# One stage of a two-block transformer kernel: running sums as rows by transfer instead of by matrix products, and another order of the work around them

## What is computed

```python
z, xbc, dt_raw, q, k, v, f_raw, g_ssd, g_att = split(h @ w_in)
# branch 1: chunked state-space product, 16 heads, 4 groups, chunk L = 128, two chunks
xbc = silu(conv(xbc)); xs, bm, cm = split(xbc); dt = softplus(dt_raw + dt_bias)
a_cs = cumsum(dt * A)                                  # within a chunk, per head
decay = exp(where(causal, a_cs[l] - a_cs[s], -inf))    # 128 x 128 per head and chunk
y_diag = ((cm . bm) * decay) @ (x * dt)
states = bm' @ (x * dt * exp(a_cs[-1] - a_cs));  y_off = (cm @ prev) * exp(a_cs)
y = y_diag + y_off + d_skip * x
y_ssd = (rms(y * silu(z)) * ssd_norm_w) @ w_ssd_o
# branch 2: forgetting attention, 8 heads of 64, query blocks of 128
F = cumsum(log_sigmoid(f_raw + forget_b))
o = softmax(q.k / 8 + F[t] - F[s], s <= t) @ v;  y_att = o @ w_att_o
out = (sigmoid(g_ssd) * y_ssd + sigmoid(g_att) * y_att) @ w_o
```

## Time and profile before

| | |
|---|---|
| median of 3 runs (lowest, highest) | 2125.88 us (2124.75, 2131.48) |
| the profiled execution, its time | 2127.87 us |
| its span, first to last instruction | 2126.1 us |
| TensorE busy | 1608.8 us, 76% of the span |
| VectorE, ScalarE, POOL busy | 419.5, 284.0, 60.2 us |
| bytes moved | 670.53 MB, mean 315 GB/s |
| mean granted TensorE clock | 0.875 of full speed |

### The profile page before, as it was taken

The page is one execution under the profiler, slowest core; times in us unless marked ns, Lnnn a source line. Parts: engine busy times, 40 slices in busy tenths (PEclk is TensorE's granted clock), DMA queues, the critical chain, the costliest instruction groups (busy, mean ns, idle before and its releaser), DMA issues.

```text
span 2126.1 us, 19636 instructions
## 1 busy us (share of the span) xinstructions
PE 1608.8 (76%) x8021; PEld 826.0 (39%) x8021; DVE 419.5 (20%) x912; ACT 284.0 (13%) x632; POOL 60.2 (3%) x79
## 2 busy tenths in 40 slices
PE   7999999799998999999999644555455446544544
PEld 3674654344443676777644311211131112211111
DVE  5521642422213122121325200000000000000001
ACT  6211222110001222222133100000000000000000
POOL 2000000000000100111100000000000000000000
PEclk9999999889999999999999776777687777877778
DMA  9999232849998642445427599999999999999996
GB/s 353 353 374 348 90 101 80 346 188 418 426 427 306 248 158 80 137 141 178 141 91 309 210 428 428 428 428 428 428 428 427 428 427 428 427 428 427 428 428 269
DMA packets 104236, 670.53 MB, mean 315 GB/s; under 512 B 8227, under 2 KB 10984, under 8 KB 71120
## 3 DMA queue, kind: packets, MB, share of 16 engines
q1 hardware_dynamic: 100000, 657.63, 75.9%
q0 software_dynamic: 3712, 11.11, 1.6%
q10 hardware_dynamic: 432, 0.49, 0.1%
HBM read 661.86 MB, written 7.34 MB: 315 GB/s over the span
## 4 chain that ended last, share of the span: by engine, by line
PE 62%; DMA 32%; DVE 2%; ACT 2%; SPq 1%; issue 1%; DVEq 0%; ACTq 0%
PE psum L1098 14%; PE psum L1087 12%; DMA ring<-in_w_up 11%; DMA ring<-in_w_down 11%; PE psum L1698 11%; DMA ring<-in_w_gate 9%; PE psum L1433 5%; PE psum L1465 3%; PE psum L1349 2%; PE psum L1400 2%; PE psum L1053 2%; PE psum L1179 1%; PE psum L1472 1%; SPq L785 1%; PE psum L1557 1%
## 5 line engine op out<-in xcount | busy, mean ns | idle before, releaser
L1698 PE MATMUL psum<-work,prob 128*32 128x512 f32 x1024 | 294.2, 739 | 162.2 <-DMA ring<-in_w_up 85.0
L1698 PE MATMUL psum<-ring,prob 128*32 128x512 f32 x1024 | 294.3, 739 | 140.9 <-DMA work<-in_w_up 82.5
L1098 PE MATMUL psum<-ring,hT 128*128 128x512 f32 x672 | 302.6, 596 | 5.0 <-ACT hT L181 4.2
L1087 PE MATMUL psum<-hT,ring 128*128 128x256 f32 x1152 | 270.4, 381 | 3.7 <-DMA ring<-in_w_in 1.7
L1087 PEld LDWEIGHTS psum<-hT,ring 128*128 128x128 f32 x1152 | 210.5, 190 | 37.3 <-issue 6.8
L1698 PE MATMUL psum<-work,hT 128*32 128x512 f32 x512 | 140.6, 711 | 83.8 <-DMA ring<-in_w_down 83.8
L1698 PE MATMUL psum<-ring,hT 128*32 128x512 f32 x512 | 140.6, 711 | 54.0 <-DMA work<-in_w_down 52.4
L1098 PEld LDWEIGHTS psum<-ring,hT 128*128 128x128 f32 x672 | 123.1, 192 | 137.1 <-issue 131.1
L1698 PEld LDWEIGHTS psum<-work,prob 128*32 128x32 f32 x1024 | 71.3, 132 | 268.5 <-issue 268.5
L1698 PEld LDWEIGHTS psum<-ring,prob 128*32 128x32 f32 x1024 | 71.4, 132 | 247.8 <-issue 246.8
L181 ACT ACTIVATE work<-psum 128x512 f32<-128x512 f32 (+2 forms) x99 | 57.1, 577 | 643.0 <-PE psum L1712 315.7
(11 more groups left out here) (334 smaller groups left out, 1424.4 us busy)
## 6 DMA issues: line engine op xcount, KB each, us to landing
work<-in_w_up SPq DMA_DIRECT2D x40, 2048.0 KB, 20.1
ring<-in_w_up SPq DMA_DIRECT2D x40, 2048.0 KB, 20.2
ring<-in_w_gate SPq DMA_DIRECT2D x38, 2048.0 KB, 19.2
work<-in_w_gate SPq DMA_DIRECT2D x38, 2048.0 KB, 19.6
work<-in_w_down SPq DMA_DIRECT2D x38, 2048.0 KB, 20.2
ring<-in_w_in SPq DMA_DIRECT2D x72, 1024.0 KB, 7.3
ring<-in_w_down SPq DMA_DIRECT2D x34, 2048.0 KB, 21.2
ring<-in_w_mod SPq DMA_DIRECT2D x24, 1024.0 KB, 13.3
```

What stands on the lines that cost most here:

```text
L1087: mm = pe.matmul(o[:, wide(j * S, S)], w[:, ch], actT[:, c, :], start=(c == 0), stop=(c == KC - 1))
L1098: mm = pe.matmul(o, lhs, w, start=(c == 0), stop=(c == KC - 1))
L1698: mm = pe.matmul(o[wide(i * CAP2, CAP2), :], lhs(chunks_per * piece + c, i), R.slot(l + i, (chunks_per, width))[:, c, wide(b * BANK, BANK) ...
```

## The change

Running sums by transfer. A new job `cum_rows` right behind `cumsum` forms the running sums as rows (16 state-space heads on partitions 0 to 15, 8 forgetting heads on partitions 32 to 39, 256 tokens each). VectorE copies them out, POOL stores them to DRAM, waits, and broadcasts the 16 rows over all partitions with two transfers, 12 heads into `mod` and 4 into `params`. `segments` reads these in place of the PSUM bank. When `y_off` is done, POOL broadcasts the 8 forgetting rows into work space, adds the causal mask to both halves (`f_first`, `f_rows`), and the attention's VectorE step adds them; the products L1327 and L1329 are gone.

The order on TensorE: cumsum and cum_rows right after v; transposes and cb; z chunk 0 with unit 9; state; z chunk 1; y_off; y_diag 0, 1; gs 0; y_diag 2, 3; gs 1, 2; all transposes of yT; gs 3; the attention with three spreads beside units 3, 7 and 11. There are six `decay` buffers. The z products are copied plainly and Silu runs once over both tiles. The attention's fills are eight jobs of 256 columns, so each spans two units.

```diff
-        for name, col0, n in (("q", Q0, 1), ("k", K0, 1), ("v", V0, 1), ("z", Z0, 2)):
-            plan_chunks(name, w_in, col0, n, IN_UNITS[name])
+        for name, col0 in (("q", Q0), ("k", K0), ("v", V0)):
...
+        jobs("cumsum", 1)
+        jobs("cum_rows", 1)
         jobs("xs_tok", 4)
         jobs("b_tok", 1)
         jobs("cb", TT)
-        for k in range(3):
-            jobs(f"a_row{k}", 1)
+        plan_chunks("z", w_in, Z0, 1, IN_UNITS["z"])
         jobs("state", 2)
-        plan_gs(0)
+        plan_chunks("z", w_in, Z0, 2, (), 1)
...
+        GS_AFTER = {1: (0,), 3: (1, 2)}
         for m in range(2 * TT):
             jobs(f"y_diag{m}", 1)
-            for k in range(3 + 2 * m, min(5 + 2 * m, TT * GROUPS)):
-                jobs(f"a_row{k}", 1)
-            if m < 3:
-                plan_gs(m + 1)
+            for j in GS_AFTER.get(m, ()):
+                plan_gs(j)
+        jobs("yT_0", 2)
+        jobs("yT_1", 2)
+        plan_gs(3)
...
-        ga_fills = chunk_fills("ga", w_in, GA0, 2)
-        fox_fills = ga_fills
-        YT_AT = {5: 0, 9: 1}
-        plan_attention("fox", FOX_UNITS, fox_fills, YT_AT)
+        fox_fills = quarter_fills("ga", w_in, GA0, 2)
+        SPREAD_AT = {3: 2, 7: 3, 11: 4}
+        plan_attention("fox", FOX_UNITS, fox_fills, SPREAD_AT)
...
+        def a_row(hd, t):
+            home = mod[:].rearrange("p a d -> p (a d)") if hd < MOD_HEADS else params[:, 1, :]
+            return home[:, wide(hd % MOD_HEADS * S + t * P, P)]
+        f_first, f_rows = view(11312, FOX_HEADS, P), view(12336, FOX_HEADS, S)
...
+            pool.wait_ge(*emptied(job("cum_rows")))
+            pool.dma_start(rows_dram[0:HEADS, :], cum_rows[0:HEADS, :]).then_inc(signal("cum_rows_stored"), 16)
+            pool.dma_start(rows_dram[wide(HEADS, FOX_HEADS), :], cum_rows[32:32 + FOX_HEADS, :]).then_inc(signal("cum_rows_stored"), 16)
+            pool.wait_ge(signal("cum_rows_stored"), 32)
+            pool.wait_ge(bias_stored[BIAS_STAGES - 1], BIAS_GROUPS // BIAS_STAGES * BIAS_STORES)
+            def spread_rows(to, first, n):
+                pool.dma_start(to, rows_dram[wide(first, n), :].rearrange("h l -> (h l)").unsqueeze(0).to_broadcast([P, n * S]))\
+                    .then_inc(signal("f_rows_in" if first == HEADS else "a_rows_in"), 16)
+            spread_rows(mod[:].rearrange("p a d -> p (a d)"), 0, MOD_HEADS)
+            spread_rows(params[:, 1, :], MOD_HEADS, HEADS - MOD_HEADS)
+            pool.wait_ge(*done(job("y_off", 1)))
+            spread_rows(f_rows.rearrange("p h l -> p (h l)"), HEADS, FOX_HEADS)
+            pool.wait_ge(signal("f_rows_in"), 16)
+            own_mask = causal[:, P:2 * P].unsqueeze(1).to_broadcast([P, FOX_HEADS, P])
+            nc.gpsimd.tensor_tensor(f_first, f_rows[:, :, 0:P], own_mask, ALU.add).then_inc(signal("f_rows_ready"), 1)
+            nc.gpsimd.tensor_tensor(f_rows[:, :, P:S], f_rows[:, :, P:S], own_mask, ALU.add).then_inc(signal("f_rows_ready"), 1)
...
+            def quarter_job(name, i, quarter):
+                k = first_job[f"{name}_{i}_{quarter}"]
+                t, part = divmod(quarter, 2)
+                o = claim(k)
+                for c, w in pieces(f"{name}_{i}") if quarter == 0 else chunks(f"{name}_{i}"):
+                    mm = pe.matmul(o[:, 0:S], class_columns(hT[:, c, :], t), w[:, wide(part * S, S)], start=(c == 0), stop=(c == KC - 1))
+                    if c < KC - 1:
+                        yield
+                finish(k, mm)
...
+            o = begin(job("cum_rows"))
+            for t in range(TT):
+                pe.matmul(o[0:HEADS, wide(t * P, P)], cum_in[:, t, 0:HEADS], tri, start=True, stop=True)
+            for t in range(TT):
+                mm = pe.matmul(o[32:32 + FOX_HEADS, wide(t * P, P)], cum_in[:, t, HEADS:24], tri, start=True, stop=(t == 0))
+            end(pe.matmul(o[32:32 + FOX_HEADS, P:S], cum_in[:, 0, HEADS:24], ones, start=False, stop=True))
...
-            for k in range(3):
-                a_row(k)
+            token_major("z", 1, hT, IN_UNITS["z"])
...
-            in_one(fill_job(gs_fills[0])[0])
+            token_major("z", 2, hT, first=1)
...
+                for j in GS_AFTER.get(m, ()):
+                    in_one(fill_job(gs_fills[j])[0])
+            transpose_tokens("yT", y_tok, "y_ssd_ready")
+            in_one(fill_job(gs_fills[3])[0])
...
-                pe.matmul(o[:, 0:n], qT[part, hd // 2, wide(t * P, P)], kT[part, hd // 2, 0:n], start=True, stop=False)
-                for s in range(t + 1):
-                    lhs = cum_in[:, s, HEADS + hd:HEADS + hd + 1].to_broadcast([P, P])
-                    mm = pe.matmul(o[:, s * P:(s + 1) * P], lhs, tri, start=False, stop=(s == t))
-                    if s < t:
-                        mm = pe.matmul(o[:, P:2 * P], lhs, ones, start=False, stop=False)
-                return mm
+                return pe.matmul(o[:, 0:n], qT[part, hd // 2, wide(t * P, P)], kT[part, hd // 2, 0:n], start=True, stop=True)
...
+            take_z(0)
+            take_z(1)
+            decay_exp(0)
+            decay_exp(1)
             act.wait_ge(signal("x_end_ready"), 1)
             for half in range(2):
                 take(job("state", half), prev[:, wide(half * BANK, BANK)])
-            def take_gate(name, j, to, which=0):
-                take(job(name, 4 * which + j), to[:, j % 2, wide(j // 2 * BANK, BANK)])
-            take_gate("gs", 0, sig_gs)
-            for k in range(3, TT * GROUPS):
-                decay_exp(k)
-                if k % 2 == 0:
-                    take_gate("gs", k // 2 - 1, sig_gs)
-            take_gate("gs", 3, sig_gs)
+            decay_exp(2)
+            decay_exp(3)
+            take_z(2)
+            decay_exp(4)
+            decay_exp(5)
+            take_z(3)
+            step(a.activation, silu_z.rearrange("p t d -> p (t d)"), silu_z.rearrange("p t d -> p (t d)"), ACT.Silu, signals=(signal("silu_z_ready"), 1))
+            logs_and_exps()
+            decay_exp(6)
+            decay_exp(7)
+            for j in range(3):
+                take_gate("gs", j, sig_gs)
...
+                if k == 0:
+                    dve.wait_ge(signal("a_rows_in"), 32)
+                if k >= DECAYS:
+                    dve.wait_ge(*done(job(f"y_diag{(k - DECAYS) // 2}")))
...
+                    step(v.scalar_tensor_tensor, decay[k % DECAYS][:, wide(r * P, P)], a_row(hd, t), a_cs[:, t, hd:hd + 1], seg_mask,
+                         ALU.subtract, ALU.add, signals=(signal("segments_ready"), k + 1) if last else None)
...
+            for k in range(1, DECAYS):
+                segments(k)
+                masked_cb(k - 1)
+                if k == 2:
+                    add_row(9)
+            masked_cb(DECAYS - 1)
             for half in range(2):
                 k = job("y_off", half)
                 take(k, v.tensor_tensor, heads_of(y_off[:, wide(half * BANK, BANK)]), heads_of(bank(k)), a_exp[:, 0, wide(half * 8, 8)].unsqueeze(2).to_broadcast([P, 8, HD]), ALU.mult)
+            segments(DECAYS)
+            segments(DECAYS + 1)
+            masked_cb(DECAYS)
+            masked_cb(DECAYS + 1)
...
+            dve.wait_ge(signal("f_rows_ready"), 2)
             def fox_mask(i, dst, src, taken):
                 hd, t = divmod(i, TT)
-                step(v.scalar_tensor_tensor, dst, src, neg_F[:, t, hd:hd + 1], causal[:, (1 - t) * P:2 * P], ALU.subtract, ALU.add, signals=taken)
-            attention("fox", FOX_UNITS, 0, fox_mask, lambda i: i % TT + 1, lambda i: o_fox[:, i % TT, wide(i // TT * FOX_D, FOX_D)], fox_fills, beside=yT_taken)
+                step(v.scalar_tensor_tensor, dst, src, neg_F[:, t, hd:hd + 1], f_rows[:, hd, :] if t else f_first[:, hd, :], ALU.subtract, ALU.add, signals=taken)
```

More of the change, by code:

```diff
@@ L390, in chunk_fills, with quarter_fills @@
             return [("chunk", name, i, half, w, col0) for i in range(n) for half in range(2)]
+        def quarter_fills(name, w, col0, n):
+            return [("chunk", name, i, quarter, w, col0) for i in range(n) for quarter in range(4)]
         def fill_span(f, fills, n):
@@ L413, in plan_attention @@
                 if i in beside:
-                    jobs(f"yT_{beside[i]}", 2)
+                    plan_spread(beside[i])
             for fill in fills:
@@ L1118, in by_tile, with token_major @@
                         in_one(token_job(name, i, t, hT))
-            def token_major(name, n, actT, units=()):
-                for i in range(n):
+            def quarter_job(name, i, quarter):
[7 more added lines that the diff above has]
+                finish(k, mm)
+            def token_major(name, n, actT, units=(), first=0):
+                for i in range(first, n):
                     for t in range(TT):
@@ L1169, in attention @@
                     if i in beside:
-                        transpose_tokens("yT", y_tok, "y_ssd_ready", (beside[i],))
+                        spread(beside[i])
             def bias(*steps):
@@ L1852, in _ @@
```

(31 more changed lines are left out.)

95 lines of the change are left out of this document (31 added, 64 removed).

## The result

| | before | changed | ratio, 95% interval |
|---|---|---|---|
| first comparison, median | 2128.6 us | 2108.99 us | 0.9908 [0.9893, 0.9923] |
| second comparison, median (five rounds) | 2128.7 us | 2112.02 us | 0.9918 [0.9904, 0.9933] |
| span of the profiled execution | 2126.1 us | 2106.1 us, second one 2110.0 us | |

A forecast was written before the change was run, and what follows sets the result against it. TensorE's own work was taken to bound the stage, bar 5.6 us of waits in the attention. Terms: -7.3 + 1.1 - 7.0 + 0.5 - 4.4 - 2.9 + 4.7 + 2.4 = -12.9 us, giving 2113.0 us; 8-in-10 range 2104 to 2121.

The forecast's parts named there:

- a_row products gone: Decay rows: 64 TensorE instructions (L1281) leave the chain of waits, -7.3 us.
- rows late: Broadcast decay rows land near 206 us, limit about 216, hidden by the z products: 0 us.
- bias products gone: Forgetting attention: products L1327 and L1329 removed, -7.0 us, bounds -7.0 and -10.2.
- waits in the attention: Even filler leaves 1.2 of 5.6 us of TensorE waits: -4.4 us, bounds 0 and -5.
- eight fills, shorter pieces: Attention filler in pieces of 256 columns, 28.2 us against 4 x 6.9 to 7.0: +0.5 us.
- clock, attention and merges: Dip at 314 goes (1.4 us), the one at the attention's end half the time: -2.9, bounds 0 and -5.2.
- gap ahead of yT: TensorE idles before the yT transposes, behind ScalarE's gs 2 copy and squares and VectorE's scaling: +4.7 us.
- clock behind it: Slower clock after TensorE's idle spell ahead of yT, sized from the gather: +2.4 us, bounds 0 and 3.5.
- the waits stay: Rival: VectorE and ScalarE set the attention's pace, or yT's wait is longer; 2120 us, chance 0.16.
- dearer parts gone: Rival: 0.2 at each score vanishes (-3.2), no clock drop at yT (-2.4), end dip goes (-1.5); 2106 us, chance 0.20.
- the switch of 0.2 us: Attention: changing from 64-row score to 128-row product costs 0.2 us, passed to whatever follows; 16 x 0.2 = 3.2 us.
- late broadcast: Rival: decay rows arrive past 216 us, each us late costing one; 2137 us if at 240, chance 0.04.

The follow-up runs named there:

- eight fills alone: Kernel before with only the gate projection ga in eight jobs of 256 columns instead of four: 2114.8 us against 2129.05, ratio 0.9939.
- the shift: Changed kernel with four of cum_rows' products made four times over, 12 more instructions at 184 us: 2110.05 us against 2129.05 before, ratio 0.9911.

## Why the prediction was right, and where its sizes were off

The direction, the mechanisms and the order of events held: the change takes TensorE's own work away, the transfers hide behind the z products, and one new gap opens. The measured times, 2109.0 and 2112.0, lie in the range, nearer to its low side than the forecast. Term by term:

| term | predicted, us | measured, us |
|---|---|---|
| a_row products gone | -7.3 | -7.4 on the chain when put back |
| cum_rows | +1.1 | +0.8 (184.15 to 184.92) |
| rows late | 0, limit 216, there at 206 | 0, limit 217.4, there at 203.4 |
| bias products gone | -7.0 | -7.1 |
| waits in the attention | -4.4 | -5.1 |
| eight fills, shorter pieces | +0.5 | about +1 |
| clock, attention and merges | -2.9 | about -5.5, by my sum below |
| gap ahead of yT | +4.7 | +4.6 |
| clock behind it | +2.4 | +1.7 and +1.8 (+2.8 in one variant) |
| moved spreads, Silu, buffers | 0 | 0 |
| stages behind the merges | 0 | -3.5 in one profile, -0.2 in the other |

The terms ahead of the last two rows sum to -12.9 as predicted and to about -17 as measured; the second merge stretch starts 16.5 us earlier in the first profile and 15.9 in the second. So the forecast of the gain was 3 to 4 us short. Some of that cancels in the time itself: it was put on a median of 2125.9 us for the kernel before, which a fourth run moved to 2128.6. That 2109 and 2112 came so near to 2113 is in part luck.

**The filler and the clock** were the mis-sized step. "The dip at 314 should go (1.4), the one at the end half the time" took 2.9 of a possible 5.2 us, 0.05 x 65.3 + 0.45 x 4.2 from the clocks of the earlier trace rows. The 2.9 was the author's estimate and no run shows it. What the runs show: before, the granted clock was 0.57 from 314 to 318 us and 0.79 in the first 9.0 us of the merges (334.4 to 343.4); with eight fills it was 1.00 in the attention and in the first merge products behind it, which took 7.08 to 7.11 us in every such variant. How that reads: in "eight fills alone" the attention and the first merge products are 7.87 + 1.89 = 9.8 us shorter; 5.2 of it is waits, and with pieces that cost about 1 more the clock gives back about 5.5 (my sum, not a measured span). The shorter pieces' price comes from the chain: 2.0 us of filler a unit after, 32.2 for 16 units, of which 3.2 is the row switch, so 29.0; before, eight units' filler at full clock is 2 x 3.44 + 6 x 3.52 = 28.0. The prediction's 28.2 for the new pieces was low.

**The waits.** The comparison with the later attention (3% idle, so 1.2 us) was cautious; 0.57 us were left. I had listed "the waits stay" with 0.16, on the ground that each spread puts 1.5 us on VectorE before the next mask. It did (two copies of 0.69 us, 277.91 to 279.46 us), and nobody waited for it.

**The gap** came at 251.5 us and took 4.58. Its slower clock behind cost 3.24 + 7.53 - 1.95 - 7.04 = 1.8 us in the first profile (granted clock 0.60 in the transposes, 0.94 in gs 3) and, in the second, 3.63 - 1.95 = 1.7, with 0.51 in the transposes and 1.00 in gs 3; with the bias products back it was 2.8 behind the same gap (clock 0.50 and 0.88). The term was taken from the gather's idle spell, and that one is a draw too: 9.16 to 10.63 us in the variants' profiles for the same 32 products. By this spread of 1.5 us I estimate that a clock term from one row carries a us of uncertainty.

**The rest of the kernel** follows the stage. In the first profile the second merge stretch starts 16.5 us earlier and the span is 20.0 shorter; the difference is the draw shown above. So the change itself is worth about 16 us, and the first median had some luck. What sets the draw isn't settled: it isn't the time at which the stages start, and no experiment here moved it on purpose.

**The rivals.** Of the three parts of "dearer parts gone" one came true (the dip at the end), the other two did not: the switch of 0.2 us stays, and the clock did drop behind the gap (0.60 in the transposes there, 1.00 where the gap was gone). The late broadcast is real but 14 us away. That rows, bias and filler each matter is shown by undoing them one by one: +7.7, +9.4, +10.2 us on the first median, +4.7, +6.4, +7.1 on the second, and by their stages 7.4, 7.1 and 5.6. The stages sum to 20.1 us; the change gained 16.5 in spite of a gap of 6.4 and 0.8 for cum_rows, 23.7 in all. What is missing, 3.6, may be yT's copies leaving the attention; no run shows it. How large the filler is depends on the rest: 9.8 us when it alone is put into the kernel before, 5.6 when it alone is taken out of the changed one.

## What to carry to other kernels

Spread filler evenly before removing work from a latency-bound loop: eight halves instead of four wholes, put alone into the kernel before, took away 5.2 us of waits and, with them, about 5.5 us of slower clock by my sum above (granted clock 0.57 from 314 to 318 us before, 1.00 with the eight), which a table of waits alone doesn't show. When a turned tile is moved ahead of a stage, write down which copy on another engine stands between its producer and its reader: here one ScalarE copy in the wrong place cost 6.5 us. And let the profile's stage lengths judge a change of a few us, as the same program ended between 2109.4 and 2114.5 us in five runs.

## What was not expected of the hardware

VectorE's products were slower beside POOL's additions. While POOL added the causal mask to the forgetting rows, two VectorE products over tiles in SBUF took 2.50 and 2.66 us, where the same product takes 0.69 a few us later. POOL's and VectorE's timelines of the changed kernel:

```profile
231.53 2.34 POOL L931 TENSOR_TENSOR work<-work,consts 128x1024 f32<-128x1024 f32 x1 [6.97 <-DMA work<-cum_rows_dram]
233.84 2.80 POOL L932 TENSOR_TENSOR work<-work,consts 128x1024 f32<-128x1024 f32 x1
```

```profile
231.92 2.50 DVE L181 TENSOR_TENSOR h_tok<-h_tok,work 128x512 f32<-128x512 f32 x1
234.53 2.66 DVE L181 TENSOR_TENSOR h_tok<-work,head_v 128x512 f32<-128x512 f32 x1
...
238.81 0.69 DVE L181 TENSOR_TENSOR h_tok<-work,head_v 128x512 f32<-128x512 f32 x1
```

The product of 231.92 ends at 234.42 and that of 234.53 at 237.19, POOL's additions at 233.87 and 236.64. With the a_row products back two products over tiles in SBUF took 2.65 and 1.93 us beside POOL's additions (238.75 to 241.26 and 241.22 to 244.01), while a product with one input in PSUM, from 241.91 us, lay wholly beside the second and kept its 0.69 us:

```profile
239.16 2.65 DVE L181 TENSOR_TENSOR h_tok<-work,head_v 128x512 f32<-128x512 f32 x1
241.91 0.69 DVE L181 TENSOR_TENSOR h_tok<-psum,h_tok 128x512 f32<-128x512 f32 x1
242.64 1.93 DVE L181 TENSOR_TENSOR h_tok<-h_tok,work 128x512 f32<-128x512 f32 x1
```

What makes the one kind slower and not the other, no run shows. The slowdown cost TensorE nothing here, since the assembly had 7 us to spare. POOL's two issues of the broadcasts took 0.57 and 0.54 us beside one VectorE product with two tensors as input (192.26 to 193.49 us); its two issues of the stores had taken 0.51 and 0.52 (from 186.46 us).

Two products into different partitions of a bank ran side by side. Of cum_rows, the head rows go to partitions 0 to 15 and the forgetting rows to 32 to 39. TensorE's timeline of the changed kernel:

```profile
184.08 0.28 PE L1298 MATMUL psum<-consts,cum_in 128*16 128x128 f32 x1
184.10 0.28 PE L1300 MATMUL psum<-consts,cum_in 128*8 128x128 f32 x1
184.20 0.27 PE L1298 MATMUL psum<-consts,cum_in 128*16 128x128 f32 x1
184.21 0.27 PE L1300 MATMUL psum<-consts,cum_in 128*8 128x128 f32 x1
```

The kernel lists all four head-row instructions ahead of the four others; in the trace they alternate, and the second of each pair starts 0.01 to 0.02 us behind the first. On the chain of waits it costs 0.01 us:

```profile
184.48 0.01 PE psum L1300
184.48 0.10 PE psum L1298
```

In the shift, 13 head-row instructions in a row, the first 12 with nothing beside them, take 1.52 us on the chain, 0.12 each. That is why the job took 0.8 us, not 1.1. That the partitions are what lets them overlap is my reading: no run put both kinds into the same ones.
